# Matrix products of ones between the routing's products, the last tile's gates added to the slot list afterwards, and the router logits one head later

## What is computed

```python
def frame_layer(x, ...):
    pr = project(x, lp)                        # RMSNorm, one combined projection
    att = attend(q, k, v, cid, ctx_cid)        # 8 heads, chunk-causal softmax attention
    hm, mstate_new = mlstm_run(mstate, mq, mk, mv, ig, logf)
    x = x + concat([att, hm]) @ w_out
    x = x + moe(rms_norm(x, g_ffn), lp)

def hier_route(xf, lp):
    g_logits = xf @ w_group + b_group          # 4 groups
    g_idx = argmax(g_logits)
    e_sel = (xf @ w_erouter + b_erouter)[group g_idx]   # 8 experts a group
    e_val, e_idx = top_k(e_sel, 2)
    gate = softmax(g_logits)[g_idx] * softmax(e_val)
    return g_idx * 8 + e_idx, gate

def moe(h, lp):                                # every token goes to 2 of 32 experts
    y[token] += gate * (silu(h[token] @ w1[e]) * (h[token] @ w3[e])) @ w2[e]
```

## Time and profile before

| | us |
|---|---|
| median of 3 runs | 1298.37 (1295.9 to 1300.96) |
| the profiled execution, its own time | 1299.81 |
| its span, first to last instruction | 1298.0 |
| TensorE busy | 1223.6 (94%) |
| VectorE busy | 421.2 (32%) |
| ScalarE busy | 335.2 (26%) |
| GpSimd busy | 279.1 (22%) |
| mean granted TensorE clock | 0.985 |

### The profile page before, as it was taken

How to read it: one execution, slowest core, us unless ns; L and a number is a source line. 1 busy time by engine, 2 the same in 40 slices (tenths; PEclk the granted TensorE clock), 3 DMA queues, 4 the chain that set the end, 5 groups by cost and what they waited for, 6 DMA issues and landing times.

```text
span 1298.0 us, 31700 instructions
## 1 busy us (share of the span) xinstructions
PE 1223.6 (94%) x13264; PEld 864.7 (67%) x13264; DVE 421.2 (32%) x926; ACT 335.2 (26%) x781; POOL 279.1 (22%) x401
## 2 busy tenths in 40 slices
PE   8999999998999999999999879998899999999997
PEld 3554444446656666766576569765599888899884
DVE  2432311016544644645443662111111111111111
ACT  3531111016334535454353310111100000000011
POOL 1320000102222222222120111322213222333321
PEclk9999999999989999999999969999999999999999
DMA  9611211134012102112030879999999999999994
GB/s 343 253 60 41 74 66 38 43 99 140 32 52 83 63 21 83 43 42 76 7 132 17 338 284 368 388 405 394 410 399 401 401 399 405 408 411 412 412 409 135
DMA packets 45260, 278.64 MB, mean 215 GB/s; under 512 B 10264, under 2 KB 15384, under 8 KB 32236
## 3 DMA queue, kind: packets, MB, share of 16 engines
q1 hardware_dynamic: 37088, 254.80, 49.0%
q0 software_dynamic: 6784, 17.84, 5.5%
q10 hardware_dynamic: 1296, 4.72, 1.0%
HBM read 250.42 MB, written 29.83 MB: 216 GB/s over the span
## 4 chain that ended last, share of the span: by engine, by line
PE 81%; issue 6%; DMA 6%; DVE 3%; ACT 2%; POOL 2%; SPq 0%; POOLq 0%; DVEq 0%; ACTq 0%
PE psum L1120 17%; PE psum L1187 16%; PE psum L1021 9%; PE psum L1252 8%; PE psum L1064 5%; PE psum L1197 4%; DMA arena<-in_w 4%; PE psum L1096 3%; PE psum L1076 2%; PE psum L894 2%; PE psum L965 2%; PE psum L1240 2%; PE psum L1179 2%; PE psum L1262 2%; PE psum L909 1%
## 5 line engine op out<-in xcount | busy, mean ns | idle before, releaser
L1187 PE MATMUL psum<-arena 128*64 128x80 f32 (+1 forms) x5632 | 231.3, 241 | 17.3 <-issue 12.8
L1120 PE MATMUL psum<-arena 128*128 128x512 f32 (+1 forms) x576 | 241.2, 577 | 4.1 <-DVE arena L1881 2.8
L1187 PEld LDWEIGHTS psum<-arena 128*64 128x64 f32 x5632 | 218.9, 138 | 29.7 <-issue 22.5
L1120 PEld LDWEIGHTS psum<-arena 128*128 128x128 f32 x576 | 108.9, 191 | 127.7 <-issue 121.5
L1021 PE MATMUL psum<-arena 128*128 128x512 f32 x288 | 126.9, 593 | 1.8 <-DVE arena L2114 1.0
L1252 PE MATMUL psum<-arena 128*64 128x80 f32 (+1 forms) x2816 | 111.5, 237 | 3.7 <-issue 2.5
L1780 POOL DMA_INDIRECT out_y<-arena,index_now x54 | 75.2, 1393 | 180.6 <-ACT arena L1598 122.5
L1252 PEld LDWEIGHTS psum<-arena 128*64 128x64 f32 x2816 | 107.1, 137 | 6.4 <-issue 4.8
L1658 POOL TENSOR_SCALAR small<-small 128x2 f32<-128x2 f32 (+4 forms) x44 | 10.4, 236 | 449.4 <-DVE small L1862 165.3
L1021 PEld LDWEIGHTS psum<-arena 128*128 128x128 f32 x288 | 53.3, 190 | 63.2 <-issue 61.5
L1598 ACT ACTIVATE arena<-psum,slot_gate 96x1024 f32<-96x1024 f32 x22 | 24.5, 1112 | 256.9 <-PE psum L1262 256.9
(11 more groups left out here) (257 smaller groups left out, 1378.2 us busy)
## 6 DMA issues: line engine op xcount, KB each, us to landing
arena<-in_w SPq DMA_DIRECT2D x94, 2048.0 KB, 19.8
z_rows<-arena SPq DMA_DIRECT2D x27, 256.0 KB, 2.0
arena<-z_rows SPq DMA_DIRECT2D x9, 768.0 KB, 5.5
arena<-in_w_in SPq DMA_DIRECT2D x3, 2048.0 KB, 21.9
arena<-in_xT_rows SPq DMA_DIRECT2D x9, 512.0 KB, 10.1
arena<-in_x_rows ACTq DMA_DIRECT2D x9, 512.0 KB, 5.5
arena<-in_x_rows SPq DMA_DIRECT2D x9, 512.0 KB, 6.7
out_y<-arena SPq DMA_DIRECT2D x9, 512.0 KB, 2.6
```

What stands on the lines that cost most here:

```text
L1120: ins = pe.matmul(o[:, 0:w], xT[n][:, k, :], w_in[:, at_ + k * w:at_ + (k + 1) * w], start=(k == 0), stop=(k == KD - 1))
L1187: ins = pe.matmul(o[c:c + CT, j * EB:j * EB + rows], w[:, k, j * P + c:j * P + c + CT], x[:, k, 0:rows], start=(k == 0), stop=(k == KD - 1))
```

## The change

Four edits. In the mixing stage `("lg", n - 1)` moves from h = 6 to h = 7, ahead of the key transposes, for n = 1 to 8. In the last tile's part of the routing VectorE only writes the token half of `tabs` (`route_places`) ahead of ranks, rows and `slot_out`; the gate half (`route_gates`) comes after `slot_out`. The last tile's two table products shrink to 32 columns, and two more products of 32 columns (`last_gates`) form its gates in bank 6, which VectorE adds to the slot list's gates after `sort_experts`. And 16 products of an all-ones matrix with 256 columns, whose results nobody reads (`keep_warm`), are put between the routing's products: three among the first 8 tiles' tables, one behind them, one behind the last tile's rank products, three behind the last tile's tables, and eight behind `last_gates`, when `tab_ok` has been waited for, ahead of the first `gather_transposes`.

```diff
@@ filler(n, h)
-        6: [("lg", n - 1)] * old + [("hsq", n)] * now + [("cn", n + 2)] * (n + 2 < NT),
-        7: [("kTa", m), ("kTb", m)] * nxt + [("hout", n)] * now,
+        6: [("lg", n - 1)] * (n == NT) + [("hsq", n)] * now + [("cn", n + 2)] * (n + 2 < NT),
+        7: [("lg", n - 1)] * (old and now) + [("kTa", m), ("kTb", m)] * nxt + [("hout", n)] * now,
@@ TensorE
                 for n in range(lo, hi):
                     for k in range(2):
-                        ins = pe.matmul(bank(2)[:, 0:2 * NE], rt["rows"][:, k * NT + n], rt["tabs"][:, k * NT + n],
+                        w = 2 * NE if n < NT - 1 else NE
+                        ins = pe.matmul(bank(2)[:, 0:w], rt["rows"][:, k * NT + n], rt["tabs"][:, k * NT + n, 0:w],
                                         start=(n == 0 and k == 0), stop=(n == NT - 1 and k == 1))
+                    if n in (1, 3, 5):
+                        keep_warm(1)
                 return ins
+            def last_gates():
+                pe.wait_ge(tail_gates, 1)
+                pe.wait_ge(read[2], ring_used[2])
+                for k in range(2):
+                    ins = pe.matmul(bank(6)[:, 0:NE], rt["rows"][:, k * NT + NT - 1], rt["tabs"][:, k * NT + NT - 1, NE:],
+                                    start=(k == 0), stop=(k == 1))
+                ins.then_inc(r_pe, 1)
+            def keep_warm(count):
+                for _ in range(count):
+                    pe.matmul(bank(0)[:, 0:2 * P], ones[:], bc1(ones[:], [P, 2, P]), start=True, stop=True)
...
             tables(0, NT - 1)
+            keep_warm(1)
             pe.wait_ge(r_dve, 2)
             pe.matmul(bank(1)[:, 0:NE], before[:], rt["m"][:, NT - 1], start=False, stop=True).then_inc(r_pe, 1)
             pe.matmul(bank(4)[:, 0:NE], ones[:], rt["m"][:, NT - 1], start=False, stop=True)
+            keep_warm(1)
             pe.wait_ge(hot_ok, 2)
             tables(NT - 1, NT).then_inc(r_pe, 1)
+            keep_warm(3)
+            last_gates()
             for b in range(4):
                 pe.wait_ge(read[b], ring_used[b])
             pe.wait_ge(tab_ok, 1)
+            keep_warm(8)
@@ VectorE
+            def route_places(lo, hi):
+                for i in range(2):
+                    TT(R["tabs"][:, i * NT + lo:i * NT + hi, 0:NE], hots[i][:, lo:hi], bc(token[:, lo:hi], [P, hi - lo, NE]), ALU.mult)
             def route_gates(lo, hi):
...
-                for i in range(2):
-                    TT(R["tabs"][:, part_(i), 0:NE], hots[i][:, lo:hi], bc(token[:, lo:hi], shape), ALU.mult)
...
                 for i in range(2):
-                    TT(R["tabs"][:, part_(i), NE:2 * NE], hots[i][:, lo:hi], bc(col(7 + i, lo, hi), shape), ALU.mult)
+                    ins = TT(R["tabs"][:, part_(i), NE:2 * NE], hots[i][:, lo:hi], bc(col(7 + i, lo, hi), shape), ALU.mult)
+                if lo:
+                    ins.then_inc(tail_gates, 1)
...
             route_tokens(NT - 1, NT)
-            route_gates(NT - 1, NT)
+            route_places(NT - 1, NT)
             route_ranks(NT - 1, NT)
             route_rows_of(NT - 1, NT)
             dve.wait_ge(r_pe, 3)
             dve.tensor_scalar(slot_out[:, 0:NE], bank(2)[:, 0:NE], NOWHERE, None, ALU.add).then_inc(tab_ok, 1)
+            route_gates(NT - 1, NT)
             link(dve.tensor_copy(R["cnt"], bank(4)[:, 0:NE]))
             link(dve.tensor_copy(slot_gate[:, 0:NE], bank(2)[:, NE:2 * NE]))
-            link(dve.tensor_copy(gate_hi[CT:CT + ET], bank(2)[0:ET, NE:2 * NE]))
             sort_experts()
+            dve.wait_ge(r_pe, 4)
+            link(TT(slot_gate[:, 0:NE], slot_gate[:, 0:NE], bank(6)[:, 0:NE], ALU.add))
+            link(dve.tensor_copy(gate_hi[CT:CT + ET], slot_gate[0:ET, 0:NE]))
```

More of the change, by code:

```diff
@@ L542, in build @@
         tab_ok, gather_idx, scatter_idx = sem("slot_tables_ready"), sem("gather_indices"), sem("scatter_indices")
+        tail_gates = sem("last_tile_gates")
         r_exp, order_ok, over_ok, over_tab = sem("route_exps"), sem("order_ready"), sem("overflow_ready"), sem("overflow_tables")
@@ L2270, in overflow_tables @@
                     TT(over_tabs[:, part_, MAX_OVER:], hot[:, part_], bc(col(7 + k), shape), ALU.mult).then_inc(hot_ok, 1)
-                dve.wait_ge(r_pe, 4)
+                dve.wait_ge(r_pe, 5)
                 toks, gates = [bank(2)[:, i * MAX_OVER:(i + 1) * MAX_OVER] for i in range(2)]
@@ L2319, in _ @@
                     if (n, h) == (NT, 2):
+                        route_places(0, NT - 1)
                         route_gates(0, NT - 1)
```

## The result

The changed kernel took 1358.8 us (median of 4 runs, 1346.5 to 1366.6) against 1299.6 us for the kernel before on the same chip (median of 4): ratio 1.045, 95% interval 1.043 to 1.048. The forecast was 1292.3 us. Its profiled execution took 1357.7 us, 57.9 more than the one of before.

A forecast was written before the change was run, and what follows sets the result against it. TensorE, busy 94%, was taken to bound the kernel, through its stream or the time until the experts' weight loads run. 1299.8 - 0.1 - 3.5 (mixing) - 3.9 (routing) = 1292.3 us; range 1289 to 1299.5.

The forecast's parts named there:

- part 4: Routing behind the slot list: at full clock the gather's transposes gain 0.6 us and the first expert's w1 product 1.7.
- Part 1: Mixing stage: logits one head later fill TensorE's wait at head 7; +0.8 for four tiles, -0.9 for tile 8: -0.1 us.
- part 2: Mixing stage: shorter rests keep TensorE's clock up in tiles 1 and 2, the rest moving to h = 6: -3.5 us.
- Rival (b): Mixing stage: rests at h = 6 let the clock fall instead, so no clock gain there: 1295.8 us, chance 0.14.
- Part 3: Routing up to the slot list: products of ones hold the clock, rank product and `slot_out` come earlier: -1.6 us.
- rival (a): Routing: clock falls among the tables all the same, slot list 3.0 us later, +2.1 instead of -3.9: 1298.3 us, chance 0.25.
- the main case: Routing: clock held from the tables to the first expert's w1 product, -3.9 us in all; forecast's chance 0.48.

The follow-up runs named there:

- e1: Kernel before plus 18 unread products of ones of 8 columns (72 instructions) on TensorE at the start: 1342.3 us against 1289.8, ratio 1.034.
- e8: Kernel before plus 136 reached waits (68 instructions) at the start of TensorE's stream: 1329.4 us in one run, before 1289.8.
- e2: Changed kernel plus 183 instructions of reached waits at the start of TensorE's stream, 256 more than before: 1308.9 us, ratio 1.014.
- e5: Changed kernel plus 183 instructions of reached waits, spread over the projection stage: 1293.1 us, ratio 1.001.
- e14: Changed kernel plus 56 instructions of reached waits, spread over the projection stage: 1292.3 us, ratio 1.003.
- e6: Changed kernel with four instead of eight products of ones ahead of the gather's transposes: ratio 1.032.
- e10: Kernel before plus the gates behind the slot list and 8 products of ones, some placed earlier; logits not moved: ratio 1.025 over the lower two of four runs.
- e3: Kernel before with only the logits moved one head later, no instruction added: ratio 1.003.
- e11: Kernel before plus the gates behind the slot list, and logits one head later in tiles 1 and 2 alone: ratio 1.000.
- e12: Kernel before plus gates behind the slot list, 8 products of ones, and logits one head later in tiles 1 and 2 (e10 and e11 together): ratio 1.031.
- e16: e12 plus 88 instructions of reached waits, spread over the projection stage: ratio 1.001 against the kernel before.
- e13: Kernel before plus 24 instructions of reached waits, spread over the projection stage: 1291.6 us in one run, before 1290.4.
- e9: Kernel before plus 129 instructions of reached waits, spread over the projection stage: 1308.1 us in one run against 1301.2.
- e4: Changed kernel without its 16 products of ones; logits' move and gates behind the slot list stay: 1289.6 us, ratio 1.001.

## Why the prediction was wrong

**The sum's missing term.** The step that failed is the price of the added work, at the end of part 4: "Without their cover the 16 products would cost 6.9 us, at half clock 13.7". It priced TensorE's added instructions by the time that they run, and nothing else; that they also push all later code along by 73 instructions, and with it a loop that just fitted, was no term and no rival. In its place the runs show +59.4 us in the loop's turns of the profiled execution, all of it more than 320 us behind the last changed instruction. e1 and e8 show it with none of the change in the kernel, e2, e5 and e14 show the change without it. What could have warned: the instruction queue's line on the page (64 packets), and that between 1056 and 1263 us only one came although TensorE did some 9,800 instructions, so that six turns ran from what was held.

How much is held: seven blocks of 256 instructions do for a body of 1621, and eight don't. Counted in the traces of e1, e6, e8, e10 and the changed kernel, the second gap comes at place 226 each time (from place 139 behind 87 instructions, from 171 behind 55), so blocks begin there (by my count, which begins at the program's first instruction); a start at 226 to 255 or 0 to 141 is a body in seven blocks. The runs agree but for place 139, which ends 2 instructions short of the seventh's end and refetches; 122, 19 short, doesn't. I read this as a few instructions being read ahead; no run shows that directly, and how many is bounded by these two alone. The Trainium skill ("Runtime: NRT & Kernel Launch", Instruction fetch mechanics) states 16 KB blocks, a store of 128 KB for TensorE (2048 instructions, eight blocks), and that a taken branch whose target isn't in a window of two blocks stalls until it is fetched. The packets of 16 KB and the stall at the branch agree with it. The window doesn't: before, the branch goes back 1621 instructions six times without a fetch. Nor does the whole store: by eight blocks every start would do, and those that touch the eighth refetch. The page would have named the rival, not its limit. Open stays why eight blocks are one too many, why the second turn never fetches again (the first loop, of two turns, doesn't either at place 140 in e14), and why two to four of the five turns behind it do; the changed kernel's runs (1346 to 1367 us) may differ by that number, but only one of them was profiled.

**Part 1 and 2, mixing stage (forecast -3.6).** From tile 0's to tile 8's last transposes (L1105, L1123 in the changed kernel) the profiled execution took 409.1 us against 412.5, -3.5 us. The stretch of tile 1 at the lower level shrank from 6.8 us to this, and the one of tile 2 (3.4 us) is gone:

```profile
358.80:362.20 3.40, 3.40 (x12) 2.20 (x11) 0.89 (x2) 1.17 (x3) 2.19 (x5) 0.50 0.36 125
```

Together 6.8 us fewer are at half clock, worth at most 3.4 us, so the gain is mostly the clock's. The waits mostly changed place, as part 2 had it for tiles 1 to 3, and in the other tiles too. Waits of TensorE from 300 to 750 us, before and changed (L1096 and L1114 are the values, L1094 the transposes of the probabilities, L1076 before):

```profile
PE psum L1096 <- ACT arena L1525: 0.9, 1, 0.9
```

```profile
PE psum L1114 <- ACT arena L1547: 10.6, 9, 1.7
PE psum L1094 <- ACT arena L1527: 1.0, 3, 0.6
```

Ahead of the transposes TensorE waits 1.0 us instead of 9.7, ahead of the values 10.6 instead of 0.9: 11.6 in all against 10.6. The -3.5 us are as forecast, but by chance. In the seven profiled executions with the whole move this stretch took 409.1, 411.1, 411.1, 414.6, 415.1, 417.0 and 418.6 us; in the eight with the logits at head 6, 412.4 to 414.1. Rival (b), the rest at head 6 letting the clock fall instead, holds in four of the seven, with some 13.6 us each at the lower level: e3, e5 and e14 in tile 3, e2 in tile 2 (from 412.6 us, behind a rest of 1.66 us), and e3 and e11 show no gain. To call it one rival of chance 0.14 was an error: the same mixing stage has it in some executions and not in others. No kernel was profiled twice, but the ten runs of e3 alone lie 10.7 us apart and those of e5 15.2, those of before on the same chip some 5. With the logits of tile 3's turn left at head 6 (e11, e12, e16) no profile has the fall in tile 3, but e12 has it in tile 2, where they were still moved:

```profile
395.70:409.30 13.60, 13.46 (x57) 9.91 (x54) 5.88 (x17) 4.11 (x12) 4.96 (x10) 0.50 0.47 158
```

**Part 3, up to the slot list (forecast -1.6), and part 4 (-2.3).** In the changed kernel's profile rival (a) came: the slot list 2.8 us later (rival: 3.0), the w1 product's end 35.0 - 33.7 = 1.3 us later (rival: 2.1). In e14 the main case came: `slot_out` at 762.41 - 745.87 = 16.54 us behind the first rank product against 761.25 - 743.19 = 18.06, -1.5; the w1 product's end at 775.62 - 745.87 = 29.75 against 33.70, -3.95 where -3.9 was forecast. So the steps of the sum were right for either course of the clock, and the course changes between profiled executions of the same work: held in e5 and e14, lost among the tables in the changed kernel and e2. Over the runs this gains nothing that can be measured (e5, e14). Part of it is given back behind the routing: counted from the second of the ranks' products, e14 is 4.8 us ahead of e13 (same chip) at the second gather's transposes (29.2 us against 34.0) and 2.1 us at the fourth (67.5 against 69.6). What takes it there wasn't tried. The other 2.1 us go against the mixing stage, which took 415.1 us in e14 and 412.5 in e13: the two executions took 1291.9 and 1291.6 us.

**The eight products ahead of the gather's transposes.** In e14 the transposes start at 768.04, 4.40 us behind the gather's issue at 763.64; before, it was 767.02 - 762.48 = 4.54. The products were cover there, not cost. In the changed kernel (issue at 759.83) it was 5.39 us, so with the clock rising late they held the transposes up by some 0.9 us. The transposes take 0.83 to 0.88 us at clock 1.00, as in the trace of before.

## What to carry to other kernels

Where an engine runs a hardware loop whose body comes near to what it holds, every instruction added or removed ahead of the loop is a change to the loop: count the packets of the instruction queue before and after, and look for idle time put down to "issue" right behind the backward branch. Padding with reached waits under long products (about free in e13, e14 and e5, 80 ns each when bare) moves the loop and so tests this in one run. A clock that falls in one execution and holds in the next can't be booked as a gain from one profile: take several of the same kernel first.

## What the runs showed of the hardware

- A taken branch back into 1621 instructions cost nothing in all six turns at places 98, 107, 122 and 227, and 11 to 15 us in each of two to four turns at 139 to 171; 9 packets of 16 KB in such a turn.
- A refetching turn has two idle gaps of TensorE (5.29 and 4.12 us at 1089), and the granted clock is 0.50 for some 10 to 14 us from within the first gap (1092.7 to 1106.3 us in the first such turn).
- A bare instruction of two reached waits takes TensorE's sequencer 80 ns (e2: 183 in 14.69 us).
- The same kernel differs by some 10 us between chips (kernel before: 1289.8, 1289.8, 1290.4, 1299.6 and 1301.2 us in the comparisons). Part of it lies in the expert stage: the turn from 1069.5 us takes 30.8 us in e13, where before has 1290.4, and the one from 1062.6 us takes 34.4 in e9, where before has 1301.2.
- The same rest ahead of the same products can be followed by either clock: 1.45 us at head 6 of tile 3 by 0.50 in e3, by 1.00 in e4.
